# Branch B's causal mask: a 64-column matmul per score block, or a VectorE write into PSUM

## The reference, cut to what matters

```python
def one_block(args):
    qn, qr, blk = args
    s = (jnp.einsum('bqhd,bkhd->bhqk', qn, k_nope)
         + jnp.einsum('bqhd,bkd->bhqk', qr, k_rope)).astype(jnp.float32) * scale
    q_chunk = (blk * Q_BLOCK + jnp.arange(Q_BLOCK)) // CHUNK
    allowed = k_chunk[None, :] <= q_chunk[:, None]
    s = jnp.where(allowed[None, None], s, MASK_VALUE)
    p = jax.nn.softmax(s, axis=-1)
    return jnp.einsum('bhqk,bkhd->bqhd', p.astype(v.dtype), v)
```

## Time and profile before

| | |
|---|---|
| median of 3 runs | 690.36 us (690.25 to 690.42) |
| the profiled execution, its own time | 690.95 us |
| its span in the trace | 689.2 us |
| TensorE matmul busy | 679.9 us, 99% of the span |
| VectorE, ScalarE, GpSimd busy | 323.4, 303.2, 303.5 us |

### The profile page before, as it was taken

One profiled execution on the slowest core, in us unless ns is written; L12 is line 12 of the kernel. 1 busy time (PEld: TensorE's weight loads), 2 busy tenths in 40 slices (PEclk: granted clock), 3 DMA queues, 4 the chain that ended last, 5 costly groups with the idle time before them and its releaser, 6 DMA issues.

```text
span 689.2 us, 9051 instructions
## 1 busy us (share of the span) xinstructions
PE 679.9 (99%) x3296; PEld 568.4 (82%) x3296; DVE 323.4 (47%) x535; ACT 303.2 (44%) x574; POOL 303.5 (44%) x145
## 2 busy tenths in 40 slices
PE   9999999999999999999999999999999999999995
PEld 8888888888888888888888888888888888888884
DVE  6857131988853533543434667777752200101013
ACT  7723232322244564564465475666853331312233
POOL 0044443544254342442442434646885384474630
PEclk9999999999999999999999999999999999999999
DMA  8732322232132122222322313112123833222215
GB/s 322 233 110 102 98 91 92 92 121 92 62 122 93 61 89 65 92 86 68 95 89 66 121 62 121 40 54 84 40 92 118 310 122 123 92 91 91 92 49 226
DMA packets 21878, 73.54 MB, mean 107 GB/s; under 512 B 2385, under 2 KB 2641, under 8 KB 21713
## 3 DMA queue, kind: packets, MB, share of 16 engines
q1 hardware_dynamic: 18144, 65.61, 28.3%
q10 hardware_dynamic: 3696, 7.43, 2.9%
HBM read 68.83 MB, written 4.19 MB: 106 GB/s over the span
## 4 chain that ended last, share of the span: by engine, by line
PE 93%; DVE 3%; ACT 2%; POOL 1%; issue 0%; ACTq 0%; POOLq 0%
PE bank L1069 28%; PE bank L1073 28%; PE bank L1072 28%; PE bank L1328 1%; DVE cqs_lo L885 1%; PE bank L1216 1%; PE bank L1202 1%; PE bank L1106 1%; PE bank L1201 1%; PE bank L1311 1%; POOL w_lo L284 1%; PE bank L1310 1%; ACT w_hi L365 1%; PE bank L1092 1%; PE bank L1089 1%
## 5 line engine op out<-in xcount | busy, mean ns | idle before, releaser
L284 POOL TENSOR_TENSOR w_lo<-w_raw,w_hi 128x1024 fp32r<-128x1024 f32 x100 | 243.6, 2438 | 329.6 <-ACT w_hi L365 329.6
L365 ACT ACTIVATE w_hi<-w_raw 128x1024 fp32r<-128x1024 f32 x110 | 116.4, 1059 | 214.4 <-PE bank L1069 178.6
L1069 PE MATMUL bank<-x_hi,w_hi 128*128 128x512 f32 x504 | 197.7, 392 | 0.0
L1073 PE MATMUL bank<-x_lo,w_hi 128*128 128x512 f32 x504 | 196.7, 390 | 0.0
L1072 PE MATMUL bank<-x_hi,w_lo 128*128 128x512 f32 x504 | 196.4, 390 | 0.0
L1073 PEld LDWEIGHTS bank<-x_lo,w_hi 128*128 128x128 f32 x504 | 94.6, 188 | 19.9
L1069 PEld LDWEIGHTS bank<-x_hi,w_hi 128*128 128x128 f32 x504 | 94.8, 188 | 19.0 <-DVE mixed L891 0.5
L1072 PEld LDWEIGHTS bank<-x_hi,w_lo 128*128 128x128 f32 x504 | 94.7, 188 | 18.7
L1069 PE MATMUL bank<-w_hi,mx_hi 128*128 128x512 f32 x256 | 101.0, 394 | 0.0
L1072 PE MATMUL bank<-w_hi,mx_lo 128*128 128x512 f32 x256 | 100.0, 391 | 0.0
L1073 PE MATMUL bank<-w_lo,mx_hi 128*128 128x512 f32 x256 | 99.9, 390 | 0.0
(11 more groups left out here) (215 smaller groups left out, 960.6 us busy)
## 6 DMA issues: line engine op xcount, KB each, us to landing
w_raw<-w_stream SPq DMA_DIRECT2D x110, 512.0 KB, 3.3
y<-x_nat ACTq DMA_DIRECT2D x4, 1024.0 KB, 9.3
out<-y SPq DMA_DIRECT2D x6, 512.0 KB, 3.3
xs<-x_t SPq DMA_DIRECT2D x4, 512.0 KB, 5.2
mixed<-x_t SPq DMA_DIRECT2D x4, 512.0 KB, 5.2
fw<-final_w ACTq DMA_DIRECT2D x1, 1024.0 KB, 15.3
cos_b<-tables ACTq DMA_DIRECT2D x2, 256.0 KB, 2.7
sin_b<-tables ACTq DMA_DIRECT2D x2, 256.0 KB, 3.0
```

Of the source, the lines that this page charges most:

```text
L284: pool.tensor_tensor(w_lo[:, s % HL, :], w_raw[:, s % RAW, :], w_hi[:, s % HL, :].bitcast(F32), ALU.subtract)\
L365: act.activation(w_hi[:, s % HL, :], w_raw[:, s % RAW, :], ACT.Copy).then_inc(w_hi_ready, 1)
L1069: ins = pe.matmul(dst, ah, bh, start=start, stop=False)
L1073: return pe.matmul(dst, ah, bl, start=False, stop=stop)
```

## The change

The mask's matmul goes. `b_scores` is counted by the last matmul of `three`. VectorE, before each maximum, writes the mask's value over the 64 x 64 block of hidden scores (partitions 0 to 63, the last 64 columns), counts a new semaphore `b_masked`, and waits for it before it takes the maximum. The small tile of mask values keeps only what mixer A uses, and so two of VectorE's first memsets go.

```diff
@@ -147,7 +147,7 @@
-        mask_bf = at("mask_bf", [P, 2, 2, CHUNK], BF16, region(512))
+        mask_bf = at("mask_bf", [P, 2, CHUNK], BF16, region(256))
@@ -649,11 +649,8 @@
             dve.memset(ones[:, :], 1.0).then_inc(consts_set, 1)
-            dve.memset(mask_bf[:, :, :, :], 0.0).then_inc(consts_set, 1)
-            dve.wait_ge(consts_set, 3)
-            dve.memset(mask_bf[:, 0, :, :], MASK_VALUE)
-            dve.memset(v_t[:, 0:CHUNK], 0.0)
-            dve.memset(mask_bf[0:64, 1, :, :], MASK_VALUE).then_inc(consts_set, 1)
+            dve.memset(mask_bf[:, :, :], MASK_VALUE).then_inc(consts_set, 1)
+            dve.memset(v_t[:, 0:CHUNK], 0.0).then_inc(consts_set, 1)
@@ -935,6 +932,9 @@
                 n = P * (u % 4 + 1)
                 dve.wait_ge(b_scores, w + 1)
+
+                dve.memset(B[4 + u % 2][0:CHUNK, n - CHUNK:n], MASK_VALUE).then_inc(b_masked, 1)
+                dve.wait_ge(b_masked, w + 1)
                 dve.reduce_max(st_b[:, u % 4, 0:1], B[4 + u % 2][:, 0:n], AX.X, negate=True).then_inc(b_max, 1)
@@ -1203,7 +1203,7 @@
-                    ins = pe.matmul(none, ident_bf[:, :], mask_bf[:, 0, :, :], start=False, stop=True)
+                    ins = pe.matmul(none, ident_bf[:, :], mask_bf[:, :, :], start=False, stop=True)
@@ -1309,9 +1309,7 @@
-                three(dst, qn_hi[par][:, h, q], qn_lo[par][:, h, q], kn_hi[par][:, h, 0:n], kn_lo[par][:, h, 0:n], False, False)
-
-                pe.matmul(B[4 + w % 2][:, n - CHUNK:n], ident_bf[:, :], mask_bf[:, 1, 0, :], start=False, stop=True).then_inc(b_scores, 1)
+                three(dst, qn_hi[par][:, h, q], qn_lo[par][:, h, q], kn_hi[par][:, h, 0:n], kn_lo[par][:, h, 0:n], False, True).then_inc(b_scores, 1)
```

More of the change, by code:

```diff
@@ L243, in build @@
         b_rot_evac, b_rot, b_rot_hi, b_rot_lo = sem("b_rot_evac"), sem("b_rot"), sem("b_rot_hi"), sem("b_rot_lo")
-        b_scores, b_max, b_exp, b_recip, b_probs = sem("b_scores"), sem("b_max"), sem("b_exp"), sem("b_recip"), sem("b_probs")
+        b_scores, b_masked, b_max, b_exp, b_recip, b_probs = sem("b_scores"), sem("b_masked"), sem("b_max"), sem("b_exp"), sem("b_recip"), sem("b_probs")
         b_turned, b_pt_hi, b_pt_lo, b_pv, b_out = sem("b_turned"), sem("b_pt_hi"), sem("b_pt_lo"), sem("b_pv"), sem("b_out")
```

## The result

| | before | changed |
|---|---|---|
| median | 690.36 us (7 runs, 690.20 to 691.41) | 692.78 us (7 runs, 692.71 to 693.06) |
| ratio to before | | 1.0033, 95% interval 1.0024 to 1.0042 |
| span of the profiled execution | 689.2 us | 690.9 us |
| TensorE, VectorE busy | 679.9, 323.4 us | 677.6, 328.4 us |

A forecast was written before the change was run, and what follows sets the result against it. Mixer B was taken as bounded by TensorE's stream and the ring scores, maximum, exponential, multiplication, transposes at once. 19 memsets at 0.17 us less 1.64 gave +1.6 us, from 690.36 to 692.0 us, range 689.9 to 694.0.

The forecast's parts named there:

- d: In mixer B, VectorE's added time per unit, for one memset and its wait: 0.17 us, between 0.07 and 0.255.
- TensorE sheds 0.12 us a mask, 0.08 behind 128 columns: In mixer B's TensorE stream, removing masks sheds 0.12 us in 24 units, 0.08 in 8; 3.6 us at most.
- Only 0.8 us of the relief counts: Of TensorE's 3.6 us relief in mixer B, 0.25 in pair 0 and 0.57 in pair 3 are left.
- the walk with d = 0: Lateness followed through mixer B's four pairs, summing to 19d - 1.64 us, here with nothing added on VectorE.
- The memset takes 0.13 and its wait 0.04, d = 0.17: On VectorE before each maximum of mixer B: 0.13 us for the PSUM write, 0.04 for its semaphore, 0.17 per unit.
- A transpose can start about 0.13 us behind its multiplication: On TensorE in mixer B: this delay leaves T3 and T6 of the first pair no margin, T6 of middle pairs 0.33.
- About 19 units pay: In mixer B, 19 of 32 memsets are paid for, each at d; sum 19d - 1.64 = +1.6 us.
- Pairs 1 and 2, each of units 2 to 7 adds d: In the middle pairs VectorE's lateness grows by d per unit: 7d - 0.33 = 0.87 us, then 7d - 0.44 = 0.75.
- Pair 3, VectorE follows TensorE: In the last pair TensorE regains 0.20 us, VectorE follows, adds 2d; 0.37 comes back: 2d - 0.57 = -0.23 us.
- A: Rival: in mixer B the memset is hidden and TensorE's full relief of 3.6 us stays, 686.8 us; chance 0.12.
- B: Rival: VectorE's wait for its own memset is free, d is 0.07, 690.05 us, no change; chance 0.15.
- C: Rival: VectorE's write into PSUM is dearer than any read, or told late; d of 0.3 gives 694.4 us; chance 0.11.

## Why the prediction was right

The direction, the range and the mechanism in its main line held; the median came out 0.8 us above the forecast. Several terms were off, with both signs, and that the total came so near is in part luck. Both things by which the prediction said it would be wrong came true: d was not 0.17, and VectorE's lateness did not add up over units 2 to 7 of the middle pairs.

- *TensorE sheds 0.12 us a mask, 0.08 behind 128 columns.* Right: 0.13 and 0.07 to 0.08 in the rows. The page "VectorE: DVE Perf Modes" of the Trainium skill, in The TRN2 errata, would have made it 0.03; the changed trace speaks against that once more.
- *Only 0.8 us of the relief counts.* Right in total. Both masks together cost 0.8 us more than VectorE's alone, and in the first and last pair only. No mask at all wins 1.84 in mixer B where the walk with d = 0 gives 1.64, but there two errors meet: 0.5 us more in the third pair, 0.3 less in the last.
- *The memset takes 0.13 and its wait 0.04, d = 0.17.* Here the size was off. The memset was 0.11 and the wait 0.03, but the price left out that an instruction placed between two that overlap loses their overlap, 0.08. d was 0.25.
- *A transpose can start about 0.13 us behind its multiplication, so T3 of the first pair has no margin.* Right for T6 (0.15 where it waits), too much for T3, which starts 0.06 behind where it waits, in the changed kernel too (422.06 + 0.75 = 422.81, and 422.86). So T3 had a margin of 0.06 us in the first pair; in the last, where it started 0.06 behind before, it had none. This was too small to change the picture.
- *About 19 units pay.* Right on average, by runs with different d. With d worked out in each from multiplication 2 to 3 of the first pair, mixer B's growth was -1.84 (no memset), 1.68 (0.19), 2.44 (0.25) and 6.03 us (0.43): from the first to the last 7.87 / 0.43 = 18. From each to the next it is 19, 13 and 20; each run also meets GpSimd at other moments, which would be enough for such a spread. With the true d, 19d - 1.64 would have been 3.1. Measured was 0.2 less in the first pair, 0.6 and 0.5 less in the middle ones and 0.6 more in the last, 2.4 in all, by what follows.
- *Pairs 1 and 2, each of units 2 to 7 adds d.* The totals were met, 0.86 and 0.82 us for 0.87 and 0.75, by two errors against each other. d was larger, and VectorE's lateness did not add up throughout. In pair 1 it went from TensorE's 0.23 at the start to 1.37 at multiplication 7, which is 4.6 d and not 7 d. In either pair two instructions that read two tiles in SBUF, the rotary split and a rotary sum, end with GpSimd's instruction and not with VectorE's own queue. Being late, VectorE meets less of it there. In pair 1 the rotary split was 1.73 us before and 1.40 after, and the sum 1.79 and 1.54.
- *Pair 3, VectorE follows TensorE.* This step failed. Forecast was -0.23, measured +0.53. Of the 0.76 between, 0.59 is the longer split (1.85 for 1.26), and 2 x 0.08 the larger d of units 2 and 3. Holding GpSimd back took away 0.90 us in the trace and 1.1 in the median. The walk has no term for GpSimd: it left the length of VectorE's splits as it was, without a reason.

On that meeting the page "SBUF — State Buffer" of the Trainium skill says, in "SBUF: two separate sides", that VectorE and GpSimd share a port pair under an exclusive lock, for which a VectorE operation with two SBUF inputs competes with a GpSimd one that reads SBUF, and that the loser fully blocks. This case's rows agree: 0.69 us when it meets nobody, 1.26 behind one GpSimd instruction, 1.85 when it just missed the gap between two. The runs show the meeting and its price; that a port is the reason is the page's word. Of the rivals, A (the relief stays) is refuted by the run without a mask. B (the wait is free) is refuted by the rows: 0.03 us behind the memset's end, and 0.20 for a second memset. C (a write into PSUM is dear) was wrong for the duration, 0.112 in both memories, and had a little truth in that a write into PSUM starts 0.05 us later.

Left open: why a memset into PSUM starts 0.05 us later than one into SBUF, and as much later behind another memset than a maximum does (0.08 and 0.03); why one into SBUF still loses 0.03 of the overlap; and why T3 needs 0.06 us behind its multiplication and T6 0.15.

## What to carry to other kernels

An engine that is busy for 99% of a stretch can still be tied to another: before work is moved off it, look how long after its releaser each of its waiting instructions starts, and count as won only what stands where that margin is wide. Price an inserted instruction from the start of the one ahead of it to the start of the one behind, the lost overlap with it, and not by its duration. Take the margin from a place where the instruction really waits, not from the smallest distance seen. Move work unit by unit, by margins: 14 of 32 moved won 1.5 us where 32 of 32 lost 2.4. And look for a third engine that shares a resource with the one on the ring, since a shift of a few tenths decides whom it meets.

## What was not expected of the hardware

- VectorE's scalar-tensor-tensor on 64 x 512 with two SBUF inputs lasted 0.69 us in one place and 1.26, 1.45 or 1.85 in others, set by where it fell in GpSimd's instructions; where it was held, it ended 0.55 us after GpSimd's did.
- VectorE's memset of 64 columns has the same row, 0.112 us, in PSUM and SBUF, but behind an instruction of 0.41 us it starts after 0.42 us with its target in PSUM and after 0.37 in SBUF, where a maximum started after 0.34.
- A 64-column bfloat16 matmul costs 0.12 us in a stream of 512-column float32 ones, and a 128-column float32 matmul makes the one behind it slow by 0.06 us too (0.29 in place of 0.23).
